# One fused decoder-layer kernel: the last group of the attention stage, with the current-token product, the branch-B norm sums and two gate sigmoids placed differently

## The chip, the cores and the metric

The kernel runs on one core of one Trainium2 chip, in one launch. The metric is the device time of that launch in microseconds (us), lower is better. Its engines are named as the profile names them: PE is TensorE, PEld its weight loads, DVE VectorE, ACT ScalarE, POOL GpSimd, SP SyncE.

## What is computed

One decoder layer on a prompt group of 256 tokens and a sample group of 8 sequences with one new token each, so T = 264 columns. Cut to what the change touches:

```
h = mod2(rms_norm(x));  qA,kA,vA,qB,kB,vB,gA,gB = split(h @ w_in)
o_a = block-sparse attention, 8 heads of 64       (prompt and sample)
o_b = differential attention, 4 heads, values 128 (prompt and sample)
o_b = rms_norm(o_b, subln_diff) * (1 - lam_init)
y_a = o_a @ w_branch_moba;  y_b = o_b @ w_branch_diff
x = x + g2 * ((sigmoid(gA) * y_a + sigmoid(gB) * y_b) @ w_out)
```

A feed-forward block stands before and after this. All data is fp32. The sample group reads 1024 cached tokens per sequence through a page table; its new token's own value row is added with its softmax weight.

## The kernel before, in words

Each engine runs one instruction stream written out by hand, and semaphores tie them together. Nothing is reordered by a scheduler: what stands first in a stream is issued first, and an instruction that waits holds up all behind it on its engine.

Big products are split: a weight block lands in `raw`, ACT copies its rounded part to `whi` (`hi(n, t)`, L723), DVE writes the rest to `wlo` (`lo(n, t)`, L1069), and PE runs three products for each 128x128 tile against `hhi` and `hlo`. `n` numbers the weight blocks: the gate blocks are `W_GATE + s`, then come four blocks of the two branch matrices (`W_BR + q`, q 0 and 1 branch A, 2 and 3 branch B), then four of `w_out`. In the attention stage the gate blocks' halves are computed by `gate_half` (L1972 to L1974).

The stage that changes is the loop `for c in range(KC)`, eight groups. In PE's stream group c holds, in this order:

- for each of two halves, the value products of the sample group (L2007): per cache (A and B) four matmuls of 512 columns, each with 32 weight columns, so that matmul q writes PSUM partitions 32q to 32q+31. In groups 1 to 6 a gate half stands between the two;
- in groups 3 and 7 the product of the current token (L2024). `dcur` has the weights of the 8 new tokens, `vtoks` their values; the result is added to the same PSUM banks 4 and 5. Call it the current-token product. DVE waits for its end (`s_pvd`) to write `om`, and PE waits for `om` (`s_om`) before the eight products of L2069, which add up the four partition groups and extract the sample output. Because these sum over all four groups, a column's share may sit in any of them;
- the transposes of the prompt's probabilities (L2037), the scores of group c + 1 (L1923, L1924), a second gate half, and the prompt's value products (L2061, L2062).

Groups 4 to 7 are branch B and need its norm. ACT squares each group's output into `osq` (L1007) and raises `s_pout`. `o_sum(c)` (L1990) sums the squares over partitions with a 128x128 matrix of ones; it waits for `s_pout` c + 1 and, for groups 5 and 6, for `s_ovar` c - 4, since they reuse PSUM bank 7. `o_variance(..., count)` on DVE (L1485, L1486) waits for the sum, scales it and takes the reciprocal. ACT takes the root later (`root`, L744).

ACT's stream in group 7: `hhi` of branch A (L986), one half of `hi(W_BR + 1)`, the copy `pts` of the turned probabilities (L995), for which PE's value products wait, then the output copies. `sigmoid(0)` and `sigmoid(1)` (L957) turn the first 8 gate tiles; each set of ACT functions needs a table load in front (ACT_TABLE_LOAD).

After the loop PE runs the branch blocks. The first waits for `s_olo`, which DVE raises at the end of the sample output's own chain.

Of the kernel before, what the change touches and what calls it, by code (L numbers as in the profile page):

```python
# [23 lines left out]
P = 128  # L24
D = 1024
KC = D // P
TP = 256
# [24 lines left out]
W_QK, W_KV, W_GATE, W_BR, W_OUT = 34, 38, 46, 54, 58  # L52
# [160 lines left out]
def build(nc, A, O):  # L213
    ctx = ExitStack()
    with ctx:
# [71 lines left out]
        vtoks = place("vtoks", [TS, D], where=r)  # L287
# [420 lines left out]
        def _(a):  # L708
# [4 lines left out]
            def hi(n, t, key=None, d=0):  # L713


                key = key or ("w", n)
                s = slot_of(key)
                a.wait_ge(s_raw[s], landed(key) + 16 * d)
                if not (isinstance(n, int) and n < 2):

                    recut = isinstance(n, int) and n in (W_BR, W_BR + 1, W_OUT, W_OUT + 1)
                    a.wait_ge(s_gemm, half_done(n, 1 if recut else t) - 4)
                nc.scalar.activation(half_view(whi[key[1] % 2], key, t), half_view(raw[s], key, t), ACT.Copy).then_inc(s_hi, 1)  # L723
# [255 lines left out]
            for c in range(KC):  # L979
                gated = 1 <= c <= 6  # L980
                if c == 1:
                    turned_probs(1)
                if c == KC - 1:
                    a.wait_ge(s_gemm, half_done(W_GATE + 7, 1))
                    a.wait_ge(s_pout, 4)
                    nc.scalar.activation(hhi[:, 0:4, 0:TP], qT[:, 0:4, 0:TP], ACT.Copy).then_inc(s_ohi, 1)  # L986
                    hi(W_BR + 1, 0)
                if gated:
                    gate_half(c + 1, 0)
                for h in range(2 if c < 4 else 1):  # L990
                    npp += 1
                    a.wait_ge(s_ppT, npp)
                    if c:
                        a.wait_ge(s_po, c)
                    nc.scalar.activation(pts[h][:, :], bank[:, turn_bank(c, h), 0:384], ACT.Copy).then_inc(s_pps, 1)  # L995
                if c + 1 < KC:
                    pad_weights(2 * c + 2)
                    pad_weights(2 * c + 3)
                    prompt_exp(c + 1)
                if gated:  # L1000
                    gate_half(c + 1, 1)
                a.wait_ge(s_po, c + 1)
                if c == 2:
                    nc.scalar.activation(dcur[:, :], bank[0:TS, 2, 256:384], ACT.Copy).then_inc(s_dcur, 1)
                ins = nc.scalar.activation(qT[:, c, 0:TP], bank[:, 2, 0:TP], ACT.Copy)
                if c >= 4:
                    ins = nc.scalar.activation(osq[:, c - 4, 0:TP], bank[:, 2, 0:TP], ACT.Square)  # L1007
                ins.then_inc(s_pout, 1)
                if c in EXTRA and c < KC - 1:
                    for t in range(2):  # L1010
                        hi(EXTRA[c], t)
# [2 lines left out]
            nc.scalar.activation(hhi[:, 0:4, TP:T], qT[:, 0:4, TP:T], ACT.Copy).then_inc(s_ohi, 1)  # L1014
            a.wait_ge(s_samp, 3)
            nc.scalar.activation(osq[:, :, TP:T], qT[:, 4:8, TP:T], ACT.Square).then_inc(s_osq, 1)
            hi(W_BR + 1, 1)
            a.wait_ge(s_sig, 14)
            sigmoid(0)
            sigmoid(1)  # L1020
            root(osq[:, 0:3, 0:TP], s_ovar, 3, s_orstd)
            root(osq[:, 3, 0:TP], s_ovar, 4, s_orstd)
            root(osq[:, :, TP:T], s_ovar, 5, s_orstd)
# [35 lines left out]
        def _(v):  # L1059
# [433 lines left out]
            for c in range(KC):  # L1493
                if c == KC - 1:
                    v.wait_ge(s_ohi, 1)
                    dve.tensor_tensor(hlo[:, 0:4, 0:TP], qT[:, 0:4, 0:TP], hhi[:, 0:4, 0:TP].bitcast(F32), ALU.subtract)
                if c % 4 == 3:

                    v.wait_ge(s_pvd, c // 4 + 1)
                    if c > 3:  # L1500
                        v.wait_ge(s_ext, c // 4)
                    else:
                        v.wait_ge(s_pT, 2)
                    for ab, (name, n) in enumerate((("maskA", 8), ("maskB", 4))):
                        mask = C(name).unsqueeze(2).broadcast_to([P, n, 512 // n])
                        ins = dve.tensor_tensor(om[:, ab, :].rearrange("p (h d) -> p h d", h=n), bank[:, 4 + ab, :].rearrange("p (h d) -> p h d", h=n), mask, ALU.mult)
                    ins.then_inc(s_om, 1)
                if c == 0:
                    sample_scale(1)
                if c in (5, 6):  # L1510
                    o_variance(osq[:, c - 5, 0:TP], bank[:, 7, 0:TP], c - 4)
                if c + 1 < KC:
                    prompt_logits(c + 1)
                    prompt_scale(c + 1)
                if c in EXTRA and c < KC - 1:
                    for t in range(2):
                        lo(EXTRA[c], t)
                if c == 3:
                    v.wait_ge(s_ext, 1)
                    dve.tensor_copy(qT[:, :, TP:TP + 4], bank[:, 7, 0:64].rearrange("p (f s) -> p f s", f=KC)[:, :, 0:4]).then_inc(s_samp, 1)  # L1520
# [5 lines left out]
            dve.tensor_tensor(hlo[:, 0:4, TP:T], qT[:, 0:4, TP:T], hhi[:, 0:4, TP:T].bitcast(F32), ALU.subtract).then_inc(s_olo, 1)  # L1526
            v.wait_ge(s_pout, KC)

            o_variance(osq[:, 2, 0:TP], bank[:, 7, 0:TP], 3)
            o_variance(osq[:, 3, 0:TP], bank[:, 6, 0:TP], 4)  # L1530
            lo(W_BR + 1, 0)
            o_variance(osq[:, :, TP:T], bank[:, 7, TP:TP + 32].rearrange("p (c s) -> p c s", s=TS), 5)
# [83 lines left out]
        def _(pe):  # L1616
# [377 lines left out]
            for c in range(KC):  # L1994
# [6 lines left out]
                for half in range(2):  # L2001
                    pe.wait_ge(s_wpad, 2 * c + half + 1)
                    for ab in range(2):
                        use = 16 + 2 * c + half
                        pe.wait_ge(kv_sem(ab, use), kv_landed(ab, use))
                        for q in range(4):
                            ins = mm(bank[32 * q:32 * q + 32, 4 + ab, :], wpad[half][:, q, ab, w0:w0 + 32], kv_slot(ab, use)[:, q, :],  # L2007
                                     start=(half == 0 and c % 4 == 0), stop=False)
                        ins.then_inc(s_pv, 1)
                    if half == 0 and c == 1:  # L2010
                        turn_probs(1)
                    if half == 0 and gated:
                        gate_half(c + 1, 0)
                    if half == 0 and c in (5, 6):
                        o_sum(c - 1)
                    if half == 1 and c == 0:
                        exp_sums(1)
                if c == 3:
                    pe.wait_ge(s_dcur, 1)
                if c % 4 == 3:  # L2020
                    for ab in range(2):
                        r0 = 64 * ab + 32 * (c // 4)
                        for j in range(4):
                            ins = mm(bank[32 * j:32 * j + 32, 4 + ab, P * j:P * j + P], dcur[:, r0:r0 + 32],  # L2024
                                     vtoks[:, 512 * ab + P * j:512 * ab + P * j + P], start=False, stop=True)
                    ins.then_inc(s_pvd, 1)
                for h in range(2 if c < 4 else 1):
                    pe.wait_ge(s_pscale, 2 * c + (h + 1 if c < 4 else 2))
# [8 lines left out]
                        ins = nc.tensor.transpose(bank[:, turn_bank(c, h), P * e:P * e + P], plog[h][:, P * e:P * e + P], ident)  # L2037
                    ins.then_inc(s_ppT, 1)
                    npp += 1
                if c == KC - 1:  # L2040
                    o_sum(c - 1)
                if c + 1 < KC:
                    pe.wait_ge(s_plog, 2 * c + 2)
                    if c == 0:
# [106 lines left out]
```

## Time and profile before

| | us |
|---|---|
| median of 3 runs | 754.25 |
| lowest, highest | 753.22, 756.5 |
| the profiled execution | 753.22 |
| its span (first to last instruction) | 751.5 |
| PE busy in the span | 727.2 (97%) |
| DVE, ACT, POOL busy | 462.9 (62%), 333.9 (44%), 130.4 (17%) |

The loop's groups 3 to 7 and what follows lie between 433 us and 523 us of the span. To read it, take PE's order of work first, and ask at each of its waits which other engine came last.

### The profile page before, as it was taken

The numbers are of one execution on the slowest core, as the hardware profiler recorded it, in microseconds if no ns is written. First come the engines' busy times: TensorE is split into PE (matmuls) and PEld (weight loads), VectorE is DVE, ScalarE is ACT, GpSimd is POOL, SyncE is SP. The second block draws the span as 40 slices with busy tenths as digits, with TensorE's granted clock in tenths as the row PEclk, the third lists the DMA queues.
The fourth block names the chain that finished last, engine by engine and source line by source line (L and its number), as shares of the span: only waits on it lengthen the run. The fifth ranks groups of instructions, "written<-read, shape, count | busy, mean of one in ns | idle before, by whom it ended". The sixth has DMA issues, their size and how long they took to land.

```text
span 751.5 us, 17385 instructions
## 1 busy us (share of the span) xinstructions
PE 727.2 (97%) x6756; PEld 650.5 (87%) x6756; DVE 462.9 (62%) x699; ACT 333.9 (44%) x568; POOL 130.4 (17%) x224
## 2 busy tenths in 40 slices
PE   5999999999999999999989999999989999999997
PEld 2498998999999699999886766699979999999997
DVE  1764445456354679996998665788674655545451
ACT  1553344344243543554255553685364443444431
POOL 0000000002000240697885324110000000000000
PEclk9999999999999999999999999999999999999999
DMA  9977888886995499999999999995616555554620
GB/s 353 378 265 266 321 304 294 332 289 254 406 334 171 164 407 387 369 393 373 405 403 319 406 407 412 363 360 170 224 56 206 186 169 171 192 181 155 209 72 30
DMA packets 116521, 209.57 MB, mean 279 GB/s; under 512 B 6714, under 2 KB 100186, under 8 KB 104162
## 3 DMA queue, kind: packets, MB, share of 16 engines
q1 hardware_dynamic: 106784, 159.47, 60.7%
q0 software_dynamic: 9440, 49.04, 16.4%
q8 instruction: 47, 0.77, 0.4%
q14 instruction: 24, 0.20, 0.1%
q10 hardware_dynamic: 226, 0.10, 0.0%
HBM read 205.33 MB, written 3.24 MB: 278 GB/s over the span
## 4 chain that ended last, share of the span: by engine, by line
PE 82%; DVE 6%; DMA 4%; issue 3%; ACT 2%; POOL 2%; SPq 1%; POOLq 0%; ACTq 0%; DVEq 0%
PE bank L1624 21%; PE bank L1626 20%; PE bank L1625 20%; PE bank L2007 4%; DMA early<-in_w_ada 3%; PE bank L1873 3%; PE bank L1680 2%; PE bank L1972 2%; PE bank L1973 2%; PE bank L1974 2%; DVE wlo L1069 1%; DMA kvB<-in_cache_k_diff 1%; POOL wlo L674 1%; PE bank L2037 1%; PE bank L1688 1%
## 5 line engine op out<-in xcount | busy, mean ns | idle before, releaser
L1069 DVE TENSOR_TENSOR wlo<-raw,whi 128x1024 fp32r<-128x1024 f32 (+1 forms) x177 | 208.6, 1199 | 176.1 <-ACT whi L723 173.3
L1624 PE MATMUL bank<-hhi,whi 128*128 128x264 f32 x992 | 286.5, 289 | 2.8 <-DVE hlo L1148 1.6
L1625 PE MATMUL bank<-hlo,whi 128*128 128x264 f32 x992 | 282.0, 284 | 0.0
L1626 PE MATMUL bank<-hhi,wlo 128*128 128x264 f32 x992 | 281.6, 284 | 0.0
L723 ACT ACTIVATE whi<-raw 128x1024 fp32r<-128x1024 f32 (+1 forms) x192 | 194.6, 1034 | 109.9 <-PE bank L1626 72.6
L1624 PEld LDWEIGHTS bank<-hhi,whi 128*128 128x128 f32 x992 | 187.5, 189 | 15.4 <-issue 14.4
L1625 PEld LDWEIGHTS bank<-hlo,whi 128*128 128x128 f32 x992 | 187.7, 189 | 0.0
L1626 PEld LDWEIGHTS bank<-hhi,wlo 128*128 128x128 f32 x992 | 186.8, 188 | 0.0
L1624 PE MATMUL bank<-ahi,whi 128*128 128x264 f32 x416 | 119.8, 288 | 0.7 <-DVE alo L1582 0.7
L1626 PE MATMUL bank<-ahi,wlo 128*128 128x264 f32 x416 | 118.2, 284 | 0.0
L1625 PE MATMUL bank<-alo,whi 128*128 128x264 f32 x416 | 117.6, 283 | 0.0
L1624 PEld LDWEIGHTS bank<-ahi,whi 128*128 128x128 f32 x416 | 78.3, 188 | 1.2 <-DVE alo L1582 1.0
L1625 PEld LDWEIGHTS bank<-alo,whi 128*128 128x128 f32 x416 | 78.3, 188 | 0.2
L1626 PEld LDWEIGHTS bank<-ahi,wlo 128*128 128x128 f32 x416 | 78.3, 188 | 0.0
L757 ACT ACTIVATE sil<-bank 128x528 f32<-128x528 f32 x22 | 13.5, 612 | 72.7 <-PE bank L1626 72.7
L674 POOL TENSOR_TENSOR wlo<-raw,whi 128x256 fp32r<-128x256 f32 x60 | 42.7, 743 | 3.5 <-issue 2.1
L761 ACT ACTIVATE ahi<-act 128x528 f32 (+1 forms) x22 | 14.2, 646 | 54.0 <-DVE act L1155 54.0
L480 POOL DMA_DIRECT2D kvB<-in_cache_v_diff x44 | 23.3, 529 | 38.9 <-PE bank L2007 29.2
L1972 PE MATMUL bank<-hhi,whi 128*128 128x264 f32 x96 | 28.6, 297 | 0.0
L1159 DVE TENSOR_TENSOR alo<-act,ahi 128x528 f32 (+1 forms) x22 | 15.6, 709 | 19.3 <-ACT ahi L761 19.3
L1973 PE MATMUL bank<-hlo,whi 128*128 128x264 f32 x96 | 27.2, 284 | 0.0
L1974 PE MATMUL bank<-hhi,wlo 128*128 128x264 f32 x96 | 27.2, 283 | 0.0
(286 smaller groups left out, 811.3 us busy)
## 6 DMA issues: line engine op xcount, KB each, us to landing
raw<-in_ffn_w_gate SPq DMA_DIRECT2D x22, 1024.0 KB, 5.3
raw<-in_ffn_w_up SPq DMA_DIRECT2D x22, 1024.0 KB, 5.4
raw<-in_w_ada SPq DMA_DIRECT2D x20, 1024.0 KB, 7.0
raw<-in_w_in SPq DMA_DIRECT2D x20, 1024.0 KB, 11.8
raw<-in_ffn_w_down SPq DMA_DIRECT2D x16, 1024.0 KB, 4.9
kvB<-in_cache_v_diff POOLq DMA_DIRECT2D x44, 256.0 KB, 6.5
kvA<-in_cache_v_moba SPq DMA_DIRECT2D x40, 256.0 KB, 8.6
kvA<-in_cache_k_moba SPq DMA_DIRECT2D x36, 256.0 KB, 7.0
```

Source lines behind the costliest of these rows:

```text
L480: eng.dma_start(rows_, cache[bass.ds(page, 1)].rearrange("a (j t) d -> (a j) (t d)", t=4)).then_inc(kv_sem(ab, use), 16)
L674: ins = nc.gpsimd.tensor_tensor(low[:, k:k + 2, :], full[:, k:k + 2, :], high[:, k:k + 2, :], ALU.subtract)
L723: nc.scalar.activation(half_view(whi[key[1] % 2], key, t), half_view(raw[s], key, t), ACT.Copy).then_inc(s_hi, 1)
L1069: dve.tensor_tensor(half_view(wlo[key[1] % 2], key, t), half_view(raw[s], key, t), half_view(whi[key[1] % 2], key, t).bitcast(F32), ALU.su ...
L1624: mm(out, wh, xh, start=start, stop=False)
L1625: mm(out, wh, xl, start=False, stop=False)
L1626: return mm(out, wl, xh, start=False, stop=stop)
L1873: ins = mm(bank[32 * m:32 * m + 32, b6, c0:c0 + 128].rearrange("p (q c) -> p q c", q=4), qrow[s % 2][:, 16 * ab + 4 * m + b, :], kv_slot(a ...
L1972: mm(out, wh, hhi[:, k, :], start=(k == 0), stop=False)
L1973: mm(out, wh, hlo[:, k, :], start=False, stop=False)
L1974: ins = mm(out, wl, hhi[:, k, :], start=False, stop=(k == KC - 1))
L2007: ins = mm(bank[32 * q:32 * q + 32, 4 + ab, :], wpad[half][:, q, ab, w0:w0 + 32], kv_slot(ab, use)[:, q, :], start=(half == 0 and c % 4 == ...
```

## The change

Four things are done.

1. The current-token product of groups 3 and 7 is issued per cache as one matmul of 512 columns into partitions 0 to 31, where it was four of 128 columns, one in each partition group. The cached products' last matmuls now close the accumulation of the other three groups.
2. On PE, `o_sum(5)` moves behind the second half of group 6's value products (it stood before them) and `o_sum(6)` to the middle of group 7's (it stood after the transposes of group 7).
3. On DVE, `o_variance` 1 moves from the start to the end of group 5, and `o_variance` 3 from behind the loop to the start of group 7, ahead of `om`.
4. On ACT, `sigmoid(0)` and `sigmoid(1)` move from behind the loop to group 7, ahead of `pts`; `hi(W_BR + 1, 0)` moves from there to behind the loop.

```diff
@@ ACT, group 7
-                    hi(W_BR + 1, 0)
+                    a.wait_ge(s_sig, 14)
+                    sigmoid(0)
+                    sigmoid(1)
@@ ACT, behind the loop
-            hi(W_BR + 1, 1)
-            a.wait_ge(s_sig, 14)
-            sigmoid(0)
-            sigmoid(1)
+            for t in range(2):
+                hi(W_BR + 1, t)
@@ DVE
                     dve.tensor_tensor(hlo[:, 0:4, 0:TP], ...)
+                    o_variance(osq[:, 2, 0:TP], bank[:, 7, 0:TP], 3)
...
-                if c in (5, 6):
-                    o_variance(osq[:, c - 5, 0:TP], bank[:, 7, 0:TP], c - 4)
+                if c == 6:
+                    o_variance(osq[:, 1, 0:TP], bank[:, 7, 0:TP], 2)
...
+                if c == 5:
+                    o_variance(osq[:, 0, 0:TP], bank[:, 7, 0:TP], 1)
...
-            o_variance(osq[:, 2, 0:TP], bank[:, 7, 0:TP], 3)
@@ PE
-                                     start=(half == 0 and c % 4 == 0), stop=False)
+                                     start=(half == 0 and c % 4 == 0), stop=(half == 1 and q > 0 and c % 4 == 3))
...
-                    if half == 0 and c in (5, 6):
+                    if (c, half) in ((5, 0), (6, 1), (7, 0)):
                         o_sum(c - 1)
...
-                        for j in range(4):
-                            ins = mm(bank[32 * j:32 * j + 32, 4 + ab, P * j:P * j + P], dcur[:, r0:r0 + 32],
-                                     vtoks[:, 512 * ab + P * j:512 * ab + P * j + P], start=False, stop=True)
+                        ins = mm(bank[0:32, 4 + ab, :], dcur[:, r0:r0 + 32], vtoks[:, 512 * ab:512 * ab + 512], start=False, stop=True)
...
-                if c == KC - 1:
-                    o_sum(c - 1)
```

PE's stream in group 7, before (the value products of the first half's B cache, those of the second half, the current-token product, the transposes, `o_sum(6)`):

```order
2972 L2007 MATMUL bank<-kvB_98,wpad_143 32x512 x3
2973 L2007 MATMUL bank<-kvA_96,wpad_144 32x512 [waits kv_landedA0,weights_padded]
...
2976 L2007 MATMUL bank<-kvB_99,wpad_144 32x512 x3
2977 L2024 MATMUL bank<-vtoks,dcur 32x128 x8
2978 L2037 MATMUL bank<-const,plog_129 128x128 [waits prompt_probs_ready,prompt_probs]
2979 L2037 MATMUL bank<-const,plog_129 128x128 x2
2980 L1990 MATMUL bank<-osq,const 128x256 [waits o_variance,prompt_out_ready]
2981 L2061 MATMUL bank<-pts_131,vtok 128x256 [waits prompt_out_ready,prompt_probs_ready]
```

And with the change:

```order
2972 L2009 MATMUL bank<-kvB_98,wpad_143 32x512 x3
2973 L1992 MATMUL bank<-osq,const 128x256 [waits o_variance,prompt_out_ready]
2974 L2009 MATMUL bank<-kvA_96,wpad_144 32x512 [waits kv_landedA0,weights_padded]
...
2977 L2009 MATMUL bank<-kvB_99,wpad_144 32x512 x3
2978 L2025 MATMUL bank<-vtoks,dcur 32x512 x2
2979 L2037 MATMUL bank<-const,plog_129 128x128 [waits prompt_probs_ready,prompt_probs]
2980 L2037 MATMUL bank<-const,plog_129 128x128 x2
2981 L2059 MATMUL bank<-pts_131,vtok 128x256 [waits prompt_out_ready,prompt_probs_ready]
```

`o_sum(6)`, with its wait for group 6's output (`prompt_out_ready`), now stands before the second half's value products, and eight small matmuls have become two.

DVE's stream from the end of group 5 into group 6, the difference (`wlo` is `lo(W_BR)`, the last work of group 5, and L1390 begins the logits of group 7):

```order
 L1069 TENSOR_TENSOR wlo_57<-raw_52,whi_55 128x8x128 x2
-L1485 TENSOR_SCALAR osq<-bank 128x256
-L1486 RECIPROCAL osq<-osq 128x256
 L1390 SCALAR_TENSOR_TENSOR plog_129<-const,qroot,bank 128x128
 L1390 SCALAR_TENSOR_TENSOR plog_129<-const,qroot,bank 128x256
...
 L1485 TENSOR_SCALAR osq<-bank 128x256
 L1486 RECIPROCAL osq<-osq 128x256
+L1485 TENSOR_SCALAR osq<-bank 128x256
+L1486 RECIPROCAL osq<-osq 128x256
```

The first pair has left its place behind the `lo` of group 4 and stands right before the other pair, so both run between the end of group 5 and the logits of group 7.

## Rows read from the trace of the kernel before

**Rows 1.** The page: busy time of each engine.
```profile
PE 727.2 (97%) x6756; PEld 650.5 (87%) x6756; DVE 462.9 (62%) x699; ACT 333.9 (44%) x568; POOL 130.4 (17%) x224
```
**Rows 2.** Busy time by engine, two stretches: PE, PEld, DVE, ACT, POOL, PEclk, DMA, GB/s.
```profile
440.00:484.00 44.00, 44.00 (x365) 31.55 (x358) 30.59 (x74) 20.73 (x58) 12.66 (x24) 1.00 1.00 391
...
500.00:510.00 10.00, 9.67 (x80) 9.49 (x79) 8.93 (x12) 8.41 (x10) 0.00 (x0) 1.00 0.91 323
```
**Rows 3.** PE's timeline in group 3: start, length, line, operands, records.
```profile
439.83 0.64 PE L2024 MATMUL bank<-vtoks,dcur 8*32 8x128 f32 x16
440.40 0.87 PE L2037 MATMUL bank<-const,plog 128*128 128x128 f32 x6
```
**Rows 4.** The chain that ended last, groups 6 and 7: start, length, what.
```profile
477.12 0.43 PE bank L1990 x2
477.55 1.85 PE bank L2007 x16
...
484.50 3.57 PE bank L2007 x32
488.07 0.57 PE bank L2024 x16
488.64 0.49 PE bank L2037 x3
...
489.15 0.50 ACT pts L995
...
489.69 0.70 PE bank L2061 x2
...
490.61 1.70 PE bank L2069 x16
```
**Rows 5.** DVE's timeline, groups 5 to 7; in brackets the idle time before.
```profile
474.86 2.36 DVE L1069 TENSOR_TENSOR wlo<-raw,whi 128x1024 fp32r<-128x1024 f32 x2 [0.61 <-ACT whi L723]
477.59 0.42 DVE L1485 TENSOR_SCALAR osq<-bank 128x256 f32<-128x256 f32 x1 [0.36 <-PE bank L1990]
478.05 1.75 DVE L1486 RECIPROCAL osq<-osq 128x256 f32<-128x256 f32 x1
480.77 0.74 DVE L1390 SCALAR_TENSOR_TENSOR plog<-const,qroot,bank 128x128 f32<-128x128 f32 x2 [0.97 <-PE bank L1924]
...
487.13 1.23 DVE L1496 TENSOR_TENSOR hlo<-qT,hhi 128x1024 fp32r<-128x1024 f32 x1 [0.55 <-ACT hhi L986]
488.70 1.29 DVE L1506 TENSOR_TENSOR om<-bank,const 128x512 f32<-128x512 f32 x2 [0.35 <-PE bank L2024]
```
**Rows 6.** ACT's timeline, group 7 and behind the loop.
```profile
485.77 0.37 ACT L1007 ACTIVATE osq<-bank 128x256 f32<-128x256 f32 x1
486.04 1.05 ACT L986 ACTIVATE hhi<-qT 128x1024 fp32r<-128x1024 f32 x1
...
493.74 1.28 ACT L957 ACT_TABLE_LOAD   x1
495.04 2.06 ACT L957 ACTIVATE gT<-gT 128x1056 f32<-128x1056 f32 x2
```
**Rows 7.** PE's timeline at its two waits behind the loop.
```profile
504.51 0.28 PE L1626 MATMUL bank<-hhi,wlo 128*128 128x264 f32 x1
505.12 0.36 PE L1624 MATMUL bank<-hhi,whi 128*128 128x264 f32 x1 [0.33 <-DVE wlo L1069]
...
521.17 0.28 PE L1626 MATMUL bank<-ahi,wlo 128*128 128x264 f32 x1
522.20 0.40 PE L1624 MATMUL bank<-ahi,whi 128*128 128x264 f32 x1 [0.75 <-DVE alo L1582]
```
**Rows 8.** DVE's timeline before PE's second wait.
```profile
511.63 0.70 DVE L1576 TENSOR_TENSOR gT<-bank,gT 128x528 f32<-128x528 f32 x1
...
512.99 2.35 DVE L1069 TENSOR_TENSOR wlo<-raw,whi 128x1024 fp32r<-128x1024 f32 x2
...
521.44 0.71 DVE L1582 TENSOR_TENSOR alo<-gT,ahi 128x528 fp32r<-128x528 f32 x1 [0.71 <-ACT ahi L1037]
```

## The prediction

> **What bounds the kernel now.** I read the page first, then the busy time by engine of the stage that the change touches, then PE's timeline and the chain of waits, and last DVE's and ACT's timelines beside it. PE is busy for 97% of the span [rows 1], and in the 44 us from the middle of group 3 to the end of group 6 for all of it, at the full clock (2.4 GHz) [rows 2]. So up to group 7 the end moves by whatever PE gains or loses, and work of DVE or ACT counts only where PE waits for it. Such waits come in group 7 and behind it. The chain goes through ACT's copy `pts` once [rows 4], and PE stands still twice in the branch stage: it starts its last product before block W_BR + 2 at 504.51 and the next at 505.12, then at 521.17 and 522.20 [rows 7]. Products there start 0.12 us apart (24 of them in the 2.9 us of each half block), so the two holes are 0.49 and 0.91 us. They are all that moved DVE and ACT work can give back here: 1.4 us.
>
> All sums below are in the time of the profiled execution (span 751.5, device time 753.22); the median of the runs shown lies 1.03 us above it.
>
> **The change, part by part.**
>
> *The current-token product, PE, groups 3 and 7.* Before, its eight matmuls (two records each) take 0.57 us, from 439.83 to 440.40 [rows 3], and 0.57 again in group 7 [rows 4]. What does a matmul of 512 columns with 32 weight columns cost? The value products have that shape: 16 records in 1.85 us, which is 8 matmuls of 512 columns, four at a time in four partition groups [rows 4]. So four such matmuls side by side take about 0.86 us, two passes of 0.43. The norm sum, alone over the whole array, takes 0.43 us for 256 columns in two passes [rows 4], again 0.86 for 512. Time thus goes by the columns streamed, not by how much of the array is used. The new form has one matmul for each cache, both into partitions 0 to 31, so nothing runs beside it: 2 x 0.86 = 1.72 us against 0.57. That is **+1.15 us in each of two groups**. The bounds: no dearer at all, if a lone narrow matmul were to run as one of four does by the count of its results (0.57 for the pair), and even 0.4 us cheaper if only the number of records counted (4 against 16); and 1.15 dearer. I take 1.15, since the row of the same shape and the row of a matmul that runs alone agree on it. In group 3 it lands on a PE that is never idle [rows 2], so all of it moves the end; the loads of cache blocks are issued when PE frees their slots and shift with it.
>
> *o_variance 1 and o_sum(5), group 6.* DVE's last work of group 5 ends at 474.86 + 2.36 = 477.22 [rows 5]. Then comes the moved o_variance 1: 0.46 to the reciprocal, 1.75 for it [rows 5], done near 479.4. PE now goes from the gate half straight into the value products, 477.12 to 478.97 (1.85), and then o_sum(5) waits for that variance: **a new wait of 0.43 us**. The sum itself (0.43 us) costs the same in its new place.
>
> *What is queued behind.* o_variance 2 can begin only when o_sum(5) is done, 479.40 + 0.43 = 479.83, and ends near 482.05. Before, the logits of group 7 began at 480.77, after a DVE that had idled 0.97 [rows 5]. They now begin 1.26 us later. Behind them on DVE and ACT hang the exponentials, and behind those, on ACT, the squares of group 6, whose end was 485.77 + 0.37 = 486.14 [rows 6]. It becomes 487.40. Before, nobody waited for that: o_sum(6) came at 489. Now it stands after the first half of group 7's value products. PE enters these 0.43 late, at 484.93, and is through half of them (1.75) at 486.68. **It waits 0.77 us** until 487.45, then sums (0.50 with the refill) until 487.95.
>
> *The rest of group 7.* The second half (1.83) ends at 489.78, the current-token product (1.72) at 491.50, the transposes (0.49) at 491.99. ACT meanwhile: hhi, 1.05 from 487.30 [rows 6], ends at 488.35; the table load 1.28 and two sigmoids 2.06 [rows 6] end at 491.67. So `pts` still starts when the transposes end, with 0.3 us to spare, and PE's value products start 0.54 later, at 492.55. Before, o_sum(6) stood in this hole (488.64 + 0.49 to 489.69 [rows 4]) and cost PE nothing; now the hole is empty and the sum is paid elsewhere: **+0.43 us**. The value products (0.92) end at 493.47, against 490.61 before [rows 4].
> DVE meanwhile: hlo until 489.65, o_variance 3 until 491.78, then `om` (1.29 [rows 5]) until 492.99. It is in time by 0.5 us, since PE itself is late.
>
> Up to here: 1.15 (group 3) + 2.86 (groups 6 and 7, which is 0.43 + 0.77 + 0.07 + 1.15 + 0.43) = **4.0 us lost**.
>
> *What the tail gives back.* DVE has one variance less behind the loop (2.2 us), ACT one table load and two sigmoids less (3.34), but a half of a `hi` more. The first hole, a wait for DVE's `wlo`, closes: 0.49 back. The second is a wait for the last `alo`, at the end of a DVE chain: the mix product at 511.63 and its add, two `lo` of 2.35 us from 512.99, the rest up to 521.44 + 0.71 [rows 8]. That mix waits for PE's block W_BR + 2, which ends 0.49 earlier, at 510.7; so the mix can start 0.9 us before 511.63, and what hangs behind it follows, 0.8 with the handovers. PE resumes near 521.4 instead of 522.20: **0.8 us back in all**, of at most 1.4.
>
> Sum: 4.0 - 0.8 = **+3.2 us**, 756.4 for an execution like the profiled one. On the median: 754.25 + 3.2 = 757.4.
>
> ACT's table load shows 1.28 us, and the sigmoid starts 0.02 after it [rows 6]. The Trainium skill, "ScalarE: Activation LUTs", section "What ACT_TABLE_LOAD costs", puts a switch of sets at about 2.66 us, since a drain of 1.38 comes on top of the load. By that figure the sigmoids would end at 493.05, `pts` would start 1.06 us later, and the sum would be +4.3; the trace shows no such drain at the place where the same load stands now, and I go by the row.
>
> **The rivals.**
>
> *The narrow matmul is cheap.* If it costs 0.57 as before, group 3 adds nothing, and in group 7 the transposes end at 490.84. Then ACT is last: `pts` cannot start before the sigmoids end at 491.67, and PE's value products end near 493.2, 2.6 late. Sum 2.6 - 0.8 = +1.8, 756.0. Against it: rows 4, twice.
>
> *The two waits don't appear*, because DVE gets through its two variances sooner than I chain them. Then 1.27 us of the 4.0 go, and up to 0.6 of the tail's gain might be added: +2.0 to +2.7, 756.3 to 757.0. For it: the first wait is only 0.43 us, about the error of such a chain. Against: the second follows from o_variance 2 standing between o_sum(5) and the logits, and both reciprocals are measured.
>
> *ACT becomes the bound of group 7, or the tail gives nothing back: slower.* ACT's queue has table load and sigmoids ahead of `pts`, with 0.3 us to spare. Each us that ACT is later than that goes to the end in full, and from 0.9 us too late the total passes 0.5% (3.8 us). Such a delay can come from the table switch; with 1.06 us of it the sum is +4.3, 758.5. The same side is reached if DVE's chain of the tail stays as long as it is: +4.0, 758.2. With both, +5.1, 759.3.
>
> *PE's holes close at no price*: 1.4 us at most, 752.9. That needs all of the 4.0 to be wrong.
>
> **How the numbers follow.** About 0.5% (3.8 us) is what a measurement of this kernel can tell from no change. Forecast near +3.2: 0.47; of this 0.10 may read as over 3.8, since the runs of before alone spread by 3 us. Cheap matmul: 0.08. No waits: 0.12. The slower rival: 0.27. A gain from closed holes: 0.06, of which 0.04 might read as faster by over 0.5%. That makes faster 0.04, slower 0.37 and within 0.5% 0.59. The range runs from the cheap matmul on an execution like the profiled one (753.22 + 1.8, less 0.4 for the bound where only records count) to the worst of the slower rival: 754.6 to 759.4.
>
> **What would show it.** Right: the current-token product at 1.7 us in groups 3 and 7; PE idle some 0.4 us before o_sum(5) and 0.8 before o_sum(6); an idle hole of 0.5 us before the value products of group 7; `pts` released by PE, not by ACT's own queue; no hole before W_BR + 2, and one of about half the size before the last products on `alo`. Wrong: a current-token product near 0.6 us (first rival); o_sum(6) starting right after the value products (second); a gap on ACT between its table load and the sigmoid, or `pts` right behind the second sigmoid (third). A lower granted clock after the new waits would make all of this too low; before, it stays full through the 0.49 us hole near 505 [rows 2, 7].

## The result and the profile after

| | before | changed |
|---|---|---|
| median | 754.49 us (8 runs) | 762.0 us (8 runs) |
| lowest, highest | 753.22, 757.73 | 758.42, 766.1 |
| profiled execution | 753.22 | 759.83 |
| its span | 751.5 | 758.1 |

The ratio is 1.0095 with a 95% interval from 1.0065 to 1.0125: slower by 0.65 to 1.25%. On a second chip the changed kernel had a median of 759.84, ratio 1.0072 (1.0050 to 1.0095). The forecast was +3.2 us, and 757.4.

The profiled execution is 6.6 us longer than the one of before. The page, its first line and the clock of 40 slices:

```profile
PE 730.7 (96%) x6732; PEld 651.7 (86%) x6732; DVE 462.4 (61%) x699; ACT 333.9 (44%) x568; POOL 130.5 (17%) x224
PEclk9999999999999999999999999989999999999999
```

PE issues 24 records fewer than in [rows 1] and is busy 3.5 us more. The 27th slice, at 493 to 512 us, shows a clock below full. (The slices are 19 us wide and hide shorter falls: the page of the kernel before has a 9 in all of them, and yet its clock was 0.79 in one stretch, as shown under "What the clock costs".) PE's timeline in groups 6 and 7, with the idle time before an instruction and its releaser in brackets:

```profile
480.62 0.67 PE L1992 MATMUL bank<-osq,const 128*128 128x256 f32 x2 [0.51 <-DVE osq L1486]
...
488.78 0.70 PE L1992 MATMUL bank<-osq,const 128*128 128x256 f32 x2 [0.69 <-ACT osq L1009]
...
491.26 1.90 PE L2025 MATMUL bank<-vtoks,dcur 8*32 8x512 f32 x4
493.09 0.55 PE L2037 MATMUL bank<-const,plog 128*128 128x128 f32 x3
494.22 0.70 PE L2059 MATMUL bank<-pts,vtok 128*128 128x256 f32 x2 [0.58 <-ACT pts L997]
...
494.98 3.00 PE L2067 MATMUL bank<-const,om 128*128 128x4 f32 x16
497.83 1.20 PE L1992 MATMUL bank<-osq,const 128*128 128x256 f32 x2
```

The first two lines are the two forecast waits, each with the releaser that was named: the variance of DVE, and ACT's squares. The current-token product is 1.90 us long, and the hole before the value products is idle. Then comes what was not forecast: the extraction (L2067) takes 3.00 us for the 16 records that had taken 1.85, and the norm sum behind it 1.20 against 0.68. The chain of waits of the same stretch, start and length:

```profile
491.33 1.83 PE bank L2025 x4
...
495.14 2.84 PE bank L2067 x16
497.98 1.06 PE bank L1992 x2
499.04 0.22 PE bank L1626
...
502.48 0.12 PE bank L1627
```

The branch products start 0.22 us apart and, from 502.48, 0.12. The busy time by engine says why. Columns: stretch, its length, busy time (and records) of PE, PEld, DVE, ACT, POOL, then the granted clock, the DMA share, GB/s. First the kernel before, then the changed one, each between 495 and 503 us:

```profile
495.00:503.00 8.00, 8.00 (x69) 8.00 (x68) 7.58 (x13) 7.24 (x12) 0.00 (x0) 1.00 1.03 407
```

```profile
495.00:503.00 8.00, 8.00 (x42) 7.82 (x41) 3.70 (x6) 5.45 (x9) 2.15 (x3) 0.57 0.95 352
```

A mean of 0.57 is the lower level (1.2 GHz) for most of the 8 us. ACT's timeline shows that the table load and the sigmoids were no obstacle, `pts` being released by PE:

```profile
489.69 1.28 ACT L957 ACT_TABLE_LOAD   x1
490.98 2.06 ACT L957 ACTIVATE gT<-gT 128x1056 f32<-128x1056 f32 x2
493.68 0.49 ACT L997 ACTIVATE pts<-bank 128x384 f32<-128x384 f32 x1 [0.64 <-PE bank L2037]
```

And at PE's second wait of [rows 7], the hole is now 0.52 us (528.83 - 528.19 - 0.12) where it was 0.91; the first one, before W_BR + 2, is gone:

```profile
528.19 0.28 PE L1628 MATMUL bank<-ahi,wlo 128*128 128x264 f32 x1
528.83 0.39 PE L1626 MATMUL bank<-ahi,whi 128*128 128x264 f32 x1 [0.36 <-DVE alo L1584]
```

The ledger of the two profiled executions: the end of group 7's value products lies at 495.14 against 490.61, 4.53 us lost. The last hole ends at 528.83 against 522.20, 6.63 us lost. Between the two, 0.49 + 0.39 = 0.9 us came back from the holes, so 6.63 - 4.53 + 0.9 = 3.0 us were lost there, all within the stretch at the lower clock. By its own rows: the extraction 2.84 against 1.70 (1.14), the norm sum 1.06 against 0.43 (0.63), and 15 branch products at 0.22 instead of 0.12 (1.5), 3.3 in all, about the same.

### The profile page after: what moved, and what is told of

Same layout as the page of the kernel before. It is cut to its first block, busy times and chain, and to the rows that moved or that the text cites. A ratio compares the mean times of both kernels' runs of the same rounds, so it can differ in the third digit from the quotient of the medians.

```text
span 758.1 us, 17337 instructions
## 1 busy us (share of the span) xinstructions
PE 730.7 (96%) x6732; PEld 651.7 (86%) x6732; DVE 462.4 (61%) x699; ACT 333.9 (44%) x568; POOL 130.5 (17%) x224
## 4 chain that ended last, share of the span: by engine, by line
PE 79%; DVE 8%; DMA 7%; issue 2%; ACT 2%; SPq 1%; POOL 0%; ACTq 0%; POOLq 0%; DVEq 0%
PE bank L1626 21%; PE bank L1627 20%; PE bank L1628 20%; PE bank L1682 3%; PE bank L1875 3%; DMA raw<-in_w_in 2%; DMA kvA_lent<-in_cache_v_moba 2%; PE bank L2009 2%; DMA kvA<-in_cache_k_moba 1%; PE bank L1690 1%; DMA const<-in_consts 1%; PE bank L1974 1%; SPq L480 1%; DVE wlo L1069 1%; PE bank L1975 1%
```

## The experiments

Theory A: the sum of the prediction is right up to group 7 (columns streamed, and two waits), and the rest is the clock, which falls because PE does less between group 6 and the branch stage. "Half clock" in the expectations is the lower level, 1.2 GHz. Its rivals differ in what brings the fall on: the narrow products, PE's idle time, or chance of a single execution. All ratios are against the kernel before on the same chip.

### One part alone

**d_only**: the current-token product alone.

```diff
-                        for j in range(4):
-                            ins = mm(bank[32 * j:32 * j + 32, 4 + ab, P * j:P * j + P], ...)
+                        ins = mm(bank[0:32, 4 + ab, :], dcur[:, r0:r0 + 32], vtoks[:, 512 * ab:512 * ab + 512], start=False, stop=True)
```

Expected:

> The kernel before with only the current-token product of groups 3 and 7 issued as one matmul of 512 columns per cache. Theory A (time goes by columns streamed): the pair takes 1.83 us as in the changed kernel, against 0.57, in both groups, PE is busy throughout, and the kernel is 2.5 us slower (near 757.0). Rival B (the narrow products alone also make the clock fall, with half speed for some 7 us around the sample extraction): 3 us more, near 760. Rival C (the product is cheap when nothing else is changed): under 0.7 us each, within 0.5 us of before.

Measured: median 757.32, ratio 1.0051 (1.0034 to 1.0067). PE's timeline in group 7, and the stretch behind it:

```profile
488.45 1.90 PE L2023 MATMUL bank<-vtoks,dcur 8*32 8x512 f32 x4
```

```profile
494.00:504.00 10.00, 10.00 (x69) 9.76 (x69) 9.49 (x15) 8.96 (x13) 1.43 (x2) 0.83 1.02 395
```

The product has the length that the columns give, whatever else is changed, which rules out rival C. In this execution PE was also at the lower clock for part of the stretch (0.83), though it had no new idle time. So the fall needs no new wait.

**o_only**: the norm sums of PE and the variances of DVE alone, as in items 2 and 3 of the change. Expected:

> The kernel before with only the moved norm sums of PE and variances of DVE. Theory A: PE waits about 0.5 us before the sum of group 5 and 0.7 before that of group 6, the sum no longer lies in the hole before the value products of group 7, so the value products of group 7 end about 2.1 us later; DVE's relief gives some 0.3 to 0.5 back: +1.7 us, near 756.2, at the full clock. Rival B (the waits, not the narrow products, make the clock fall): half speed after group 7 and near 759.

Measured: median 759.13, ratio 1.0073 (1.0056 to 1.0089). Theory A's +1.7 fell, its half-clock rival's 759 held. PE's waits, and the stretch behind group 7:

```profile
482.24 0.67 PE L1992 MATMUL bank<-osq,const 128*128 128x256 f32 x2 [0.51 <-DVE osq L1486]
490.40 0.70 PE L1992 MATMUL bank<-osq,const 128*128 128x256 f32 x2 [0.69 <-ACT osq L1007]
494.58 0.70 PE L2061 MATMUL bank<-pts,vtok 128*128 128x256 f32 x2 [0.58 <-ACT pts L995]
495.86 1.95 PE L2069 MATMUL bank<-const,om 128*128 128x4 f32 x16 [0.36 <-DVE om L1507]
```

```profile
494.00:504.00 10.00, 9.06 (x57) 8.57 (x58) 6.40 (x12) 7.26 (x11) 2.16 (x4) 0.83 1.04 395
```

This is the dearest single part. It has the two waits of the changed kernel to the hundredth and one more, for `om`: with the cheap product PE comes earlier than DVE, whose variance 3 now stands ahead of `om`.

**os_only**: the changed kernel with the current-token product as before. Expected:

> The changed kernel with the current-token product in four partition groups as before. Theory A: value products of group 7 end 2.1 us late, both later waits of PE shrink by 0.9 to 1.0 us in all, clock full: +1.2 us, near 755.7. Rival B (clock falls because of the waits): near 758.7, with half speed at 495 us.

Measured: median 758.36, ratio 1.0059 (1.0042 to 1.0075), lower clock behind group 7 (0.83 between 494 and 504). The half-clock rival again. Here the sigmoids do hold up `pts`:

```profile
495.23 0.70 PE L2061 MATMUL bank<-pts,vtok 128*128 128x256 f32 x2 [1.09 <-ACT pts L997]
```

**s_only**: the sigmoids alone.

```diff
-                    hi(W_BR + 1, 0)
+                    a.wait_ge(s_sig, 14)
+                    sigmoid(0)
+                    sigmoid(1)
```

Expected:

> The kernel before with only ACT changed: sigmoids 0 and 1 ahead of the copy of the turned probabilities in group 7. ACT has 1.1 us idle there before, and the table load and sigmoids take 3.34 us against 1.05 for the half of hi that leaves, so the copy starts near 490.4 instead of 489.15: PE waits 1.2 us more in group 7. The tail gives back up to 1.4 us. Theory A: between -0.2 and +0.5 us, within noise of before, 754.0 to 755.0. Rival: the longer wait makes the clock fall, +3 us.

Measured: median 756.24, ratio 1.0042 (1.0028 to 1.0056), so 2.5 us where theory A had at most 0.5. PE's wait and the clock:

```profile
491.98 0.70 PE L2061 MATMUL bank<-pts,vtok 128*128 128x256 f32 x2 [1.34 <-ACT pts L997]
```

```profile
494.00:504.00 10.00, 10.00 (x71) 9.77 (x70) 8.92 (x14) 6.38 (x12) 1.65 (x3) 0.83 1.02 404
```

**d_and_o**: the changed kernel with ACT's stream as before. Expected:

> The changed kernel with ACT's stream as before (sigmoids behind the loop). In the changed kernel the copy of the turned probabilities waits for PE and not for the sigmoids, so the loop should take the same time without them, while ACT has 3.34 us more of work behind it. Theory A: the same waits and the same 1.83 us products, half clock again; less given back behind the loop, so 0 to 0.7 us slower than the changed kernel. Rival B (the sigmoids cost time in the loop): faster than the changed kernel by about 1 us.

Measured: median 760.61, ratio 1.0089 (1.0066 to 1.0111), beside 759.84 of the changed kernel on the same chip. PE has the same waits of 0.52, 0.69 and 0.58 us. So in the changed kernel the sigmoids cost nothing in the loop, because the product's extra time covers them; alone they do cost.

### The current-token product in two partition groups

**d_two_groups**: the changed kernel, but the two caches' products write different partitions.

```diff
-                        ins = mm(bank[0:32, 4 + ab, :], dcur[:, r0:r0 + 32], ...)
+                        ins = mm(bank[32 * ab:32 * ab + 32, 4 + ab, :], dcur[:, r0:r0 + 32], ...)
```

Expected:

> The changed kernel, but the current-token product of cache B goes to partitions 32 to 63, that of cache A to 0 to 31, each still one matmul of 512 columns. Theory A (time goes by columns streamed, and different partition groups run side by side): the pair takes about 0.9 us instead of 1.83 in both groups, and the kernel is 1.9 us faster than the changed one. Rival B (lone narrow matmuls don't overlap, or different banks keep them apart): 1.8 us again and no gain.

Measured: median 756.84, ratio 1.0043 (1.0024 to 1.0063), against 1.0095 and 1.0072 of the changed kernel. PE's timeline:

```profile
490.56 1.05 PE L2025 MATMUL bank<-vtoks,dcur 8*32 8x512 f32 x4
```

The same two matmuls of the same shape, 1.05 us instead of 1.90. This shows the mechanism of the first term: they take turns only because both sit in the same partition group. Here too the clock was at 0.83 between 494 and 504, and the value products waited 0.68 us for `pts`, which now waited for the sigmoids, since PE comes to it earlier.

### What the clock costs

**before_again**: the kernel before, for a second profile. Expected:

> The kernel before, unchanged, for a second profile. If the stretch behind group 7 is always at full clock in it, the half clock there belongs to the changed versions; if it is at half clock here too, it is a matter of the single execution and the profiled one of before was lucky by 1 to 2 us.

Measured: 754.63 (one run). The stretch behind group 7:

```profile
494.00:504.00 10.00, 10.00 (x83) 9.87 (x82) 9.54 (x15) 9.23 (x14) 1.43 (x2) 1.00 1.04 408
```

Full clock again. **after_again**: the changed kernel, for a second profile. Expected:

> The changed kernel unchanged, on the same chip as its variants. Theory A: 759 to 762 us, half clock for 3.4 to 6.8 us from about 495 us, current-token product 1.83 us, waits of 0.5, 0.7 and 0.6 us. Rival: near 757, which would mean that the earlier 762 came from the chip.

Measured: median 759.84, ratio 1.0072 (1.0050 to 1.0095); waits of 0.51, 0.69 and 0.58 us, the product 1.90, and:

```profile
494.00:504.00 10.00, 9.85 (x53) 9.62 (x54) 4.54 (x9) 5.54 (x10) 2.14 (x3) 0.66 0.96 359
```

Both profiles of the changed kernel have 0.66 in this stretch, both of the kernel before 1.00. That holds for this stretch only. The kernel before falls elsewhere in both of its profiles, in code that the change does not touch, and the changed kernel does not in either of its own. First before, then the changed kernel (`after`):

```profile
386.00:394.00 8.00, 6.33 (x40) 6.31 (x41) 7.62 (x20) 6.93 (x21) 5.73 (x9) 0.79 1.02 389
```

```profile
386.00:394.00 8.00, 6.57 (x53) 6.37 (x53) 7.62 (x18) 5.53 (x16) 6.41 (x10) 1.00 1.03 390
```

So a time of the whole kernel mixes what the change does with falls that have nothing to do with it. The table at the end of this section takes them out.

**fill_holes** and **fill_again** are one kernel: the changed one with three matmuls nobody reads, put into PE's waits.

```diff
                     if (c, half) in ((6, 1), (7, 0)):
+                        pe.wait_ge(s_plog, 2 * c + 2)
+                        mm(bank[:, 1, 0:256], C("ones"), const[:, 0:256], start=True, stop=True)
...
+                if c == KC - 1:
+                    mm(bank[:, 1, 0:256], C("ones"), const[:, 0:256], start=True, stop=True)
```

Expected of fill_holes:

> The changed kernel with one matmul of 256 columns that nobody reads (0.43 us, full array, into a free bank) in front of each of the three places where PE waits: the sum of group 5, that of group 6, and the value products of group 7. The three waits are 0.51, 0.69 and 0.58 us, so the path gets at most 0.3 us longer. Theory A (the half clock comes from PE's own idle time in groups 6 and 7): full clock through the sample extraction, and 2 to 3 us faster than the changed kernel, near 759. Rival B (it comes from the narrow products and the many short ones, whatever the holes): the same half clock at about 495 us and a time at or 0.3 us above the changed kernel's 762.

Expected of fill_again:

> The changed kernel with the three fillers once more, for a second profile and beside the changed kernel on the same chip. Theory A: 757 to 758 us, 3 to 4 us faster than the changed kernel, and a shorter stretch at half clock behind group 7, or none. Rival B: the earlier gain was a matter of the chip, and both lie together.

Measured: 757.56 (756.61 to 765.69), ratio 1.0048 (1.0029 to 1.0068); and 758.56 (756.34 to 762.98), ratio 1.0059 (1.0040 to 1.0079), beside 759.84 of the changed kernel on the same chip. PE's timeline of fill_again, the filler (L2044) in the last hole, and the stretch behind:

```profile
493.89 0.55 PE L2040 MATMUL bank<-const,plog 128*128 128x128 f32 x3
494.27 0.60 PE L2044 MATMUL bank<-const 128*128 128x256 f32 x2
495.01 0.70 PE L2064 MATMUL bank<-pts,vtok 128*128 128x256 f32 x2
495.55 0.39 PE L2065 MATMUL bank<-pts,vtok 128*128 128x128 f32 x2
495.77 1.85 PE L2072 MATMUL bank<-const,om 128*128 128x4 f32 x16
```

```profile
494.00:504.00 10.00, 9.85 (x76) 9.16 (x77) 7.40 (x13) 6.07 (x11) 2.15 (x3) 1.00 0.94 324
```

More work and less time: full clock, the extraction back at 1.85 us, 757.52 for this execution. But the profiled execution of fill_holes, the same kernel, took 765.69 and was at 0.73 in that stretch, without any wait of PE in groups 6 and 7. So the fillers don't rule the fall out. The two intervals overlap those of the changed kernel; both medians lie below both of its medians. That the fillers make the fall rarer fits, and is not shown.

**wide_same_time** and **wide_again**, also one kernel: before, with PE longer by wide work.

```diff
                     ins.then_inc(s_pvd, 1)
+                    pe.wait_ge(s_plog, 2 * c + 2)
+                    for _ in range(2):
+                        mm(bank[:, 1, 0:384], C("ones"), const[:, 0:384], start=True, stop=True)
```

Expected of wide_same_time:

> The kernel before, with two matmuls of 384 columns that nobody reads, over the full array, behind the current-token product of groups 3 and 7: PE gets 1.28 us longer in each, as much as the one-matmul form adds (1.83 against 0.57), but with the whole array at work instead of 8 rows by 32 columns. Theory A (the narrow product also costs clock, beyond its own time): full clock behind group 7, +2.5 us, about 1 us less than the version with the current-token product alone changed. Rival B (any longer stretch there brings the half clock, whatever runs in it): the same half clock of 3.4 us at 494 us and the same +3.6 us.

Expected of wide_again:

> The version with wide work of the same length, once more and on the same chip. Theory A: full clock in the whole loop and behind it, +2.8 us. Rival B: half clock for 3.4 us behind group 7, and the same time as the version with the narrow product.

Expected of d_only_again, the counterpart with the narrow product on the same chip:

> The version with only the current-token product changed, once more. Theory A (the narrow product also costs clock): half clock for some 3.4 us behind group 7 again, and a time about 1 us above that of the version with wide work of the same length. Rival B (one execution was unlucky): full clock there, and the same time as with the wide work, +2.8 us.

Measured: wide work 757.22, ratio 1.0041 (1.0027 to 1.0056), then 757.38, ratio 1.0027 (1.0012 to 1.0042), full clock in the stretch both times. Narrow product again: 758.29, ratio 1.0040 (1.0021 to 1.0059), and this time full clock there as well:

```profile
494.00:504.00 10.00, 10.00 (x81) 9.70 (x82) 7.70 (x13) 7.97 (x12) 2.15 (x3) 1.00 1.04 397
```

Narrow work reads 0.10 to 0.13% above wide work of the same length, inside the intervals. That it brings on the fall by itself is not shown: one profile of two. The price of its own time is shown: 1.28 us of work added to PE in two places costs 2.0 to 3.1 us by the medians, about what the sum has (two times 1.15).

**s_fill**: the sigmoids alone, with two fillers (0.86 us) in PE's wait of 1.34 us. Expected:

> The version with only the sigmoids moved, with two matmuls of 256 columns that nobody reads (0.86 us) in PE's wait of 1.34 us for the turned probabilities. Theory A (that version's loss is half clock after the longer wait): full clock behind group 7, and 1 to 2 us faster than the 756.2 of the sigmoids alone, near 754.5. Rival B (its loss is something else, on ACT or DVE): the same 756.2.

Measured: median 755.31, ratio 1.0004 (0.9988 to 1.0020), against 1.0042 (1.0028 to 1.0056) without the fillers. The intervals are apart, but that does not show that the fillers helped. The two ran on different chips, and the one kernel that ran on the same pair of chips, d_only, also reads lower on the second: 1.0051, then 1.0040. And the profiles show no gain. That of s_fill (756.79, among the slower ones of this kernel) was at 0.83 between 494 and 504, as that of s_only was, and it was no faster in the stretch that the change touches, as the table shows. The fillers left 0.48 us of the wait.

**One stretch, in all the profiles.** No kernel differs from before ahead of group 3's current-token product (but for a flag on the matmuls right in front of it), and from the end of PE's second wait behind the loop to the end of the span every profile has 229.2 to 229.3 us. Between executions the start of that product lies anywhere from 439.02 to 444.00 us, which moves the whole time and says nothing about the change. So the time from that start to the end of the second wait is the change's own. For the kernel before it is 522.20 - 439.83 = 82.37 us. "Idle" is PE's new waits in groups 6 and 7 added up; the clock is that of 494 to 504 us.

| profile | idle | clock | start, end | length | against before |
|---|---|---|---|---|---|
| before | none | 1.00 | 439.83, 522.20 | 82.37 | |
| before_again | none | 1.00 | 441.27, 523.64 | 82.37 | 0.00 |
| the changed kernel | 1.78 | 0.66 | 439.70, 528.83 | 89.13 | +6.76 |
| after_again | 1.78 | 0.66 | 439.62, 528.76 | 89.14 | +6.77 |
| fill_again | none | 1.00 | 440.49, 526.56 | 86.07 | +3.70 |
| fill_holes | none | 0.73 | 444.00, 534.75 | 90.75 | +8.38 |
| d_and_o | 1.79 | 0.83 | 439.85, 527.38 | 87.53 | +5.16 |
| d_two_groups | 1.88 | 0.83 | 439.85, 525.88 | 86.03 | +3.66 |
| o_only | 2.14 | 0.83 | 442.58, 528.29 | 85.71 | +3.34 |
| os_only | 2.30 | 0.83 | 442.72, 528.36 | 85.64 | +3.27 |
| s_only | 1.34 | 0.83 | 440.92, 524.98 | 84.06 | +1.69 |
| s_fill | 0.48 | 0.83 | 441.75, 525.84 | 84.09 | +1.72 |
| d_only | none | 0.83 | 439.02, 524.49 | 85.47 | +3.10 |
| d_only_again | none | 1.00 | 441.49, 526.39 | 84.90 | +2.53 |
| wide_same_time | none | 1.00 | 440.32, 525.38 | 85.06 | +2.69 |
| wide_again | none | 1.00 | 442.76, 527.81 | 85.05 | +2.68 |
| table_var3 | none | 1.00 | 440.59, 522.03 | 81.44 | -0.93 |

Where no clock fell, a kernel repeats to 0.01 us (before, wide). Three things follow. First, the price of the fall: the changed kernel and fill_again both reach the extraction 55.28 us after the start of the product (before: 50.62), so the fillers cost nothing, and the 3.06 us between 89.13 and 86.07 are the fall's. In fill_holes, the same kernel as fill_again, a longer fall cost 4.68 us. Second, a fall need not cost that much: the shorter one in d_only costs 0.57 us (85.47 against 84.90), since PE, slowed down, reaches both later waits when their releasers are nearly or quite done. Third, what goes with the fall: all eight profiles with new idle time in groups 6 and 7 have it, and two of the nine without (d_only, fill_holes). Idle time is strongly tied to the fall, but is neither its only cause nor a condition of it.

### A version made to beat the kernel before

**table_var3**: PE's stream as before. DVE's variance 3 goes behind `om`, and a sigmoid of one column brings ACT's table load into its idle time.

```diff
+                if c == KC - 1:
+                    nc.scalar.activation(misc[:, 20:21], misc[:, 21:22], ACT.Sigmoid)
...
                     ins.then_inc(s_om, 1)
+                    if c == KC - 1:
+                        o_variance(osq[:, 2, 0:TP], bank[:, 7, 0:TP], 3)
```

Expected:

> A version made to beat the kernel before: the current-token product, the norm sums, the variances 1 and 2 and the sigmoids stay where they were; variance 3 moves right behind om in group 7, where DVE idles 1.45 us, and a one-column sigmoid behind the copy of the turned probabilities brings the table load (1.28 us) into ACT's 1.0 us of idle time. PE's stream is untouched. Theory A: no new wait in group 7, both later waits of PE (0.49 and 0.91 us) shrink: 0.5 to 1.2 us faster than before. Rival B: the copies of the sample output come 0.6 us later behind variance 3 and PE's first branch block with them: 0.6 us lost, nothing gained on balance.

Measured: median 753.41 (12 runs), ratio 0.9995 (0.9982 to 1.0007): no slower, and a gain that the runs can't tell from none. PE is busy 25.64 us between 504 and 530, against 24.92 in the kernel before:

```profile
504.00:530.00 26.00, 25.64 (x211) 25.41 (x210) 21.26 (x28) 14.00 (x17) 0.00 (x0) 1.00 0.65 209
```

So 0.7 us of the two holes is closed, what the changed kernel also had from its moves, here without a new wait. In the table above the stretch takes 0.93 us less than before, within the forecast 0.5 to 1.2. That is 0.1% of the time, less than executions differ by, so only the profile shows it, and one profile of this kernel is all there is.

## Why the prediction was wrong

*The current-token product.* Forecast 1.15 us more in each of two groups; 1.26 by the chain (1.83 against 0.57). Right, and d_two_groups shows the reason: columns streamed in one partition group add up. In d_only_again, at full clock, the two together cost 2.53 us, twice 1.26.

*The first wait, 0.43 us, and the second, 0.77.* 0.51 and 0.69 us. Right in place, size and releaser. Mis-sized was what comes behind a wait: from the start of each sum to PE's next instruction it is 0.50 us (480.62 to 481.12) and 0.63 (488.78 to 489.41), where the prediction had 0.43 and 0.50.

*The sum moved out of the hole, ACT's margin, `om`.* Right: 0.58 us idle, `pts` waited for PE by 0.64, and the value products were not held up by DVE.

*Up to the end of group 7's value products:* 4.0 forecast, 4.53 measured in the profiled executions, and 4.66 from the start of group 3's product on (55.28 against 50.62): 1.26 for 1.15 in group 3, 0.60 for 0.43 in group 6, 2.80 for 2.42 in group 7. The two products are 0.22 of the difference, the two waits with their sums most of the rest.

*The tail gives back 0.8.* It gave 0.9, the first hole whole and 0.39 of the second. The profile of the changed kernel alone would not show that the moved work did it, since in d_only, where DVE and ACT are as before, the fall closed the same holes. fill_again shows it: at full clock the first hole is gone as well and the second is down to 0.36 us by the profile, from 0.75.

*The clock.* This is the step that failed. The prediction closed with "before, it stays full through the 0.49 us hole near 505" and set the price of a fall to nothing, both in the sum and in the range. But that hole lies between long runs of dense products, 0.12 us apart. The new holes lie in front of a stretch in which PE has mostly short work: transposes, sixteen records of four columns, a sum. One hole of the same length in dense work was no evidence for three of them there. Nor does the prediction name a fall elsewhere, and the trace that it read has one: 0.79 between 386 and 394.

The measured price in the profiled execution is 3.06 us. Without the fall the change costs 3.70 us (fill_again), close to the 3.2 of the sum; with it 6.76, against +5.1 for the worst case that the range allows. So the sum had its steps right, but for 0.5 us, and lacked a term as large as itself.

The measured medians differ by 7.5, 0.7 more than 6.76, and on the second chip by 5.4 (759.84 against 754.39), 1.3 less. Where these differences go is not shown: the slower executions of the changed kernel were not profiled. The mean clock of the span fits in part: 758.42 at 0.997, 759.83 at 0.995, 763.53 and 763.71 at 0.987 and 0.989; but the slowest, 766.1, is at 0.991. And that mean does not tell where a fall lies: it is 0.995 in the profiled execution of the kernel before too, from falls ahead of group 3.

*The rivals.* The cheap product and the absent waits are refuted by rows. The slower rival had ACT's queue or the tail as its mechanism; neither came. It named the right side for a reason that did not happen. The rule on the table load that stood beside it was tested as well: the Trainium skill, "ScalarE: Activation LUTs", section "What ACT_TABLE_LOAD costs", has about 1.38 us of drain on top of the load. In the new place the load takes 1.28 us from 489.69 and the sigmoid starts at 490.98, so the trace shows no drain that adds time here.

What stays open: what brings the fall on. Idle time goes with it in eight profiles of eight, against two of nine without, but d_only and fill_holes fell with none. For the narrow product alone the profiles are one to one, and that fillers keep the clock up is seen in one profile of two.

## What to carry to other kernels

Fewer instructions are not less work for TensorE: four narrow matmuls side by side cost the columns of one, and put together into one wide-streaming matmul they cost all of them. Before a step is moved to an earlier place in an in-order stream, follow its wait back to the engine that ends it; a norm sum that had lain in a hole for nothing became two waits. And where TensorE's work is thin already, count every new idle spot as a risk to the clock too: here waits of 1.8 us in all went with a fall that cost 3.1 us more. Last, where executions differ by more than the change is worth, read the stretch that it touches from each profile, from the last instruction that is common to all.

## What the runs showed of the hardware

- A matmul of 512 fp32 columns with 8 rows and 32 weight columns takes as long for its columns as one over the full array: two of them in one partition group take 1.83 us in the changed kernel, 1.8 ns a column. In wide_same_time two of 384 columns over the full array take 1.40 us (440.89 to 442.29), 1.8 ns a column as well. From start to start of the next instruction the narrow pair in two partition groups takes 0.98 us (d_two_groups, 439.85 to 440.83).
- After idle spots of 0.4 to 1.3 us in a thin stretch the granted clock was 0.83 or 0.66 on average over 10 us in all eight profiles of the seven versions with such waits; in both profiles of the kernel before and both with wide work it was 1.00 there. It also fell without such waits (d_only 0.83, fill_holes 0.73), and one kernel can show either (fill_holes 0.73, fill_again 1.00; d_only 0.83, d_only_again 1.00).
- What a fall of TensorE's clock costs depends on what comes behind it. In the changed kernel (0.66 over 10 us) it cost 3.06 us; in d_only (0.83), where TensorE would have waited later on anyway, 0.57 us.
- In the changed kernel's place for them, ACT's table load takes 1.28 us and the sigmoid starts right behind it.
